# Expert stage of a transformer kernel: seven steps of 512 columns instead of fourteen of 256

## What is computed

```python
def moe_swiglu(h, w_router, w_gate, w_up, w_down):
    logits = jnp.einsum('bsd,de->bse', h, w_router).astype(jnp.float32)
    top_v, top_i = lax.top_k(logits, TOP_K)
    ...
        a = jnp.einsum('sd,edf->sef', hb, w_gate)
        u = jnp.einsum('sd,edf->sef', hb, w_up)
        act = jax.nn.silu(a) * u * gb[:, :, None]
        return jnp.einsum('sef,efd->sd', act, w_down)
```

## Time and profile before

| | us |
|---|---|
| median of 3 runs | 2570.42 |
| lowest and highest | 2569.68, 2573.59 |
| span of the profiled execution | 2562.5 |
| first to last turn of the expert stage | 725.6 to 1723.6 |

### The profile page before, as it was taken

One profiled execution on the slowest core, in us unless ns is written; L12 is line 12 of the kernel. 1 busy time (PEld: TensorE's weight loads), 2 busy tenths in 40 slices (PEclk: granted clock), 3 DMA queues, 4 the chain that ended last, 5 costly groups with the idle time before them and its releaser, 6 DMA issues. The chain is left out here.

```text
span 2562.5 us, 30519 instructions
## 1 busy us (share of the span) xinstructions
PE 2260.2 (88%) x11133; PEld 1876.1 (73%) x11133; DVE 1862.5 (73%) x1965; ACT 1343.6 (52%) x1446; POOL 54.4 (2%) x130
## 2 busy tenths in 40 slices
PE   3946899785799999999999999997879999787998
PEld 3825788673678888888887878776767878676786
DVE  6887667678589888888898888876645446555454
ACT  2423343352367777777777777763434435343443
POOL 2000000000000000000000000000000000000000
PEclk9957999896799999999999999997989999898999
DMA  8840678560179999999999999994424554231553
GB/s 297 284 156 2 211 282 289 213 208 1 49 242 349 352 348 354 351 353 349 353 348 350 344 349 346 347 344 143 157 82 148 196 175 150 99 116 66 175 174 134
DMA packets 412850, 595.07 MB, mean 232 GB/s; under 512 B 20316, under 2 KB 327751, under 8 KB 412743
## 3 DMA queue, kind: packets, MB, share of 16 engines
q1 hardware_dynamic: 407040, 586.55, 66.3%
q10 hardware_dynamic: 5702, 7.04, 0.8%
HBM read 592.47 MB, written 1.05 MB: 232 GB/s over the span
## 5 line engine op out<-in xcount | busy, mean ns | idle before, releaser
L136 PE MATMUL bank<-ring_rounded,hT_rounded 128*128 128x512 f32 (+3 forms) x944 | 373.8, 396 | 19.5 <-DVE ring_rounded L291 5.6
L693 DVE TENSOR_TENSOR ring_rounded<-ring,z_rounded 128x2048 fp32r<-128x2048 f32 x148 | 338.9, 2291 | 63.0 <-ACT z_rounded L685 61.3
L136 PE MATMUL bank<-ring_rounded,z_rounded 128*128 128x512 f32 x896 | 361.6, 404 | 3.0 <-DVE ats_rounded L2825 1.5
L693 DVE TENSOR_TENSOR ring_rounded<-ring,zT_rounded 128x2048 fp32r<-128x2048 f32 x145 | 332.3, 2292 | 42.2 <-ACT zT_rounded L685 40.8
L685 ACT ACTIVATE z_rounded<-ring 128x2048 fp32r<-128x2048 f32 x148 | 283.4, 1917 | 32.7 <-DMA ring<-in_moe_w_up 25.0
L685 ACT ACTIVATE zT_rounded<-ring 128x2048 fp32r<-128x2048 f32 x145 | 277.9, 1917 | 35.8 <-DMA ring<-in_moe_w_up 18.4
L136 PE MATMUL bank<-ring_rounded,L_rounded 128*128 128x512 f32 x712 | 282.3, 396 | 15.3 <-DVE ats_rounded L826 10.5
L137 PE MATMUL bank<-zT_rounded,ats_rounded 128*128 128x512 f32 x600 | 234.8, 391 | 0.0
L136 PEld LDWEIGHTS bank<-ring_rounded,hT_rounded 128*128 128x128 f32 x944 | 181.5, 192 | 56.0 <-issue 15.7
L136 PEld LDWEIGHTS bank<-ring_rounded,z_rounded 128*128 128x128 f32 x896 | 168.3, 188 | 41.7 <-DVE ring_rounded L693 4.3
L693 DVE TENSOR_TENSOR ring_rounded<-ring,PT_rounded 128x2048 fp32r<-128x2048 f32 x71 | 162.6, 2290 | 44.0 <-ACT PT_rounded L685 43.9
(11 more groups left out here) (491 smaller groups left out, 4876.5 us busy)
## 6 DMA issues: line engine op xcount, KB each, us to landing
ring<-in_moe_w_gate SPq DMA_DIRECT2D x224, 512.0 KB, 5.1
ring<-in_moe_w_up SPq DMA_DIRECT2D x224, 512.0 KB, 6.9
ring<-in_moe_w_down SPq DMA_DIRECT2D x224, 512.0 KB, 7.8
ring<-in_ffn_w_gate_up SPq DMA_DIRECT2D x88, 512.0 KB, 5.0
ring<-in_ffn_w_down SPq DMA_DIRECT2D x66, 512.0 KB, 7.8
ring<-in_w_ada SPq DMA_DIRECT2D x48, 512.0 KB, 6.6
ring<-in_w_in SPq DMA_DIRECT2D x32, 512.0 KB, 4.8
xn<-in_w_ada SPq DMA_DIRECT2D x24, 512.0 KB, 9.5
```

Of the source, the lines that this page charges most:

```text
L136: pe.matmul(out, r32(a[0]), r32(b[1]), start=start, stop=False, skip_group_check=True)
L693: dve.tensor_tensor(r32(w), w, high(hi), ALU.subtract).then_inc(sem_out, 1)
```

## The change

A step now covers 512 hidden columns, and there are seven per expert (56 in all, before 112). A step uses all six slots: 0 and 1 hold gate (four blocks of 128 rows, 512 columns each), 2 and 3 hold up, 4 and 5 hold two row blocks of `w_down` each. A row of a gate or up transfer is 2 KB long where it was 1 KB; a row of `w_down` stays 4 KB. PE's `into` replaces `gate_up`: gate goes to bank 6, up to bank 7, 24 products each, and the semaphore `gu` is raised once for each slot, `down` likewise. Since bank 7 also takes the transposed activation, `up` waits until that has been split (`actT`). SP waits for each slot alone. `turn` makes four transposes. The later gathers and the swap go to bank 6, so PE waits for silu before them, and for `hTb` (or `combined`) before the next gate products; they stand in steps 2 to 5 and 6 of seven. On DVE the low part of slot 0 of the next step stands ahead of the multiplication. The clearing of the output bank and the wait for `me_count` stand ahead of the first step. The loads of slots 4 and 5 of step m stand behind the four loads of step m + 1, for step 0 too. At the end, both last `w_down` slots are split behind the copy of the last turn. On PE all steps are written out; on ACT and DVE a loop runs over pairs of experts.

```diff
-MOE_STEPS = F_EXPERT // FT
+WIDE = 512
+MOE_STEPS = F_EXPERT // WIDE
+ROWS_DOWN = WIDE // P
...
+MOE_SLOTS = ('gu', 'gu', 'gu', 'gu', 'down', 'down')
+MOE_UP = 2
+MOE_ALL = MOE_STEPS * N_EXP
+def moe_use(s, m, after=0):
+    return m * (4 if s < 4 else 2) + (s % 4 + after)
...
         for a in range(2):
-            sp.dma_start(w[:, a:a + 1, :], c.moe_down[:, bass.ds(m * 2 + a, 1), :])\
+            sp.dma_start(w[:, a:a + 1, :], c.moe_down[:, bass.ds(m * ROWS_DOWN + (2 * half + a), 1), :])\
               .then_inc(sem, 16)
+    else:
+        w = w.rearrange('p (k n) -> p k n', k=4)
+        view = c.moe_gate if s < MOE_UP else c.moe_up
+        for a in (0, 2):
+            sp.dma_start(w[:, a:a + 2, :], view[:, bass.ds(e * KD + (4 * half + a), 2), bass.ds(i * WIDE, WIDE)])\
+              .then_inc(sem, 16)
...
+    def load(s, e, i, m, first=False):
         if not first:
-            sp.wait_ge(E['gu' if q < 2 else 'down'], m + (moe_before(p, 'gu') - 1))
+            sp.wait_ge(E[MOE_SLOTS[s]], moe_use(s, m, (-3 if s < 4 else -1) + moe_before(p, MOE_SLOTS[s])))
...
-        moe_load(c, sp, q, e, i, m, (j0 + 3 * r + q) % RING, (c.again if p else c.landed)[(j0 + 3 * r + q) % RING])
...
-    def step(e, i, r, m):
-        load(0, e, i, r, m)
-        load(1, e, i, r, m)
-        load(2, None, None, 1 - r, m - 1)
...
+    def step(e, i, m, first=False):
+        for s in range(4):
+            load(s, e, i, m)
+        for s in (4, 5):
+            load(s, None, None, m - 1, first)
+    for s in range(4):
+        load(s, 0, 0, 0, True)
+    step(0, 1, 1, True)
+    with sp.Fori(2, MOE_STEPS) as i:
+        step(0, i, i)
     with sp.Fori(1, N_EXP) as e:
...
-GATHER_STEP = MOE_STEPS - 6
+GATHER_STEP = 2
 GATHERS = 4
+SWAP_STEP = GATHER_STEP + GATHERS
...
-            body(i % 2, m0 + i, ahead, None if g > GATHERS else (lambda g=g: extra(e, half, g, last)))
-        if last:
-            end(e)
-            return
-        body(0, m0 + MOE_STEPS, 2, lambda: next_extra(e, half, known))
-        body(1, m0 + (MOE_STEPS + 1), 2, None)
-    for r in range(2):
-        body(r, r, 2, None)
+            more = (lambda g=g: extra(e, half, g, last)) if 0 <= g <= GATHERS else None
+            after = (lambda: boundary(e - 1, 1 - half, last)) if i == 0 and known != 0 else None
+            body(m0 + i, known == 0 and i == 0, not (last and i == MOE_STEPS - 1), more, after)
     moe_experts(eng, expert)
+    end()
...
 def later_gather(c):
-    return c.pb[7][:, S:2 * S]
+    return c.pb[6][:, 0:S]
...
-    def gate_up(half, r, m):
+    def into(first, out, half, m):
         hTe, hLe = c.hTe[half], c.hLe[half]
         for q in range(2):
-            pe.wait_ge(E['gu_lo'], moe_split_value(st, q, m, p))
...
+            wh, wl = parts(s, 4)
...
+                mm = product(pe, out[:, :], (hTe[:, x, :], hLe[:, x, :]), (wh[:, i, :], wl[:, i, :]), x == 0, x == KD - 1)
+            mm.then_inc(E['gu'], 1)
...
     def turn(m):
         pe.wait_ge(E['act'], m + (1 + moe_before(p, 'act')))
-        for a in range(2):
-            mm = pe.transpose(T[:, a * P:a * P + P], c.fa[:, 0, a * P:a * P + P], c.ident[:, :])
+        for a in range(ROWS_DOWN):
+            mm = pe.transpose(U[:, a * P:a * P + P], c.moe_fa[:, a * P:a * P + P], c.ident[:, :])
         mm.then_inc(E['turned'], 1)
...
-                             first and a == 0, last and a == 1)
-        mm.then_inc(E['down'], 1)
+        for q in range(2):
+            pe.wait_ge(E['down_lo'], moe_use(4 + q, m, 1 + moe_before(p, 'down_lo')))
+            wh, wl = parts(4 + q, 2)
+            for h in range(2):
+                col = slice(h * 512, h * 512 + 512)
+                for i in range(2):
+                    a = 2 * q + i
+                    mm = product(pe, c.pb[4 + h][:, :], (c.moe_faT[:, a, :], c.moe_faL[:, a, :]),
+                                 (wh[:, i, col], wl[:, i, col]), first and a == 0, last and a == ROWS_DOWN - 1)
+            mm.then_inc(E['down'], 1)
...
+    def swap(e):
...
         pe.wait_ge(E['sums'], e + (1 + moe_before(p, 'sums')))
...
     def expert(e, m0, half, known):
         last = known == N_EXP - 1
...
+        for i in range(MOE_STEPS):
+            m = m0 + i
+            if i == 0 and known != 0:
+                pe.wait_ge(E['hTb'], e * 4 + (4 + moe_before(p, 'hTb')))
+                pe.wait_ge(E['combined'], e + moe_before(p, 'combined'))
+            elif not last and 0 < i - GATHER_STEP <= GATHERS:
+                pe.wait_ge(E['hTb'], e * 4 + (4 + i - GATHER_STEP + moe_before(p, 'hTb')))
+            into(0, G, half, m)
+            if i or known != 0:
+                pe.wait_ge(E['actT'], m + moe_before(p, 'actT'))
+            into(MOE_UP, U, half, m)
             g = i - GATHER_STEP
-            gate_up(half, i % 2, m0 + i)
-            down(1 - i % 2, m0 + (i - 1), False, False)
...
-            turn(m0 + i)
+            if (0 <= g < GATHERS and not last) or g == GATHERS:
+                pe.wait_ge(E['silu'], m + (1 + moe_before(p, 'silu')))
+                if g < GATHERS:
+                    gather(e + 2, 1 - half, g, later_gather(c))
+                else:
+                    swap(e)
+            if i or known != 0:
+                if i == 1 and known != 0:
+                    scatter(e - 1)
+                down(m - 1, i == 1, i == 0)
+            turn(m)
         if last:
-            down(1, m0 + (MOE_STEPS - 1), False, True)
+            down(m, False, True)
             scatter(e)
-            return
-        m1 = m0 + MOE_STEPS
-        pe.wait_ge(E['hTb'], e * 4 + (8 + moe_before(p, 'hTb')))
-        gate_up(1 - half, 0, m1)
-        down(1, m0 + (MOE_STEPS - 1), False, True)
-        turn(m1)
-        gate_up(1 - half, 1, m0 + (MOE_STEPS + 1))
-        scatter(e)
...
+        gather(1, 0, g, first_gather(c, g))
     if p == 0:
         for n in range(NT):
             mm = pe.matmul(c.pb[3][:, 0:N_EXP], c.ones[:, 0:P], c.chosen[:, n, :], start=n == 0, stop=n == NT - 1)
         mm.then_inc(c.s['mo_tensor'], 1)
         moe_clear(c, pe, 2)
     pe.wait_ge(E['hTb'], 4 + moe_before(p, 'hTb'))
-    gate_up(0, 0, 0)
-    turn(0)
-    if p == 0:
-        pe.wait_ge(c.s['me_count'], 1)
-        moe_clear(c, pe, 3)
...
+    if p:
+        moe_experts(pe, expert)
+        return
+    pe.wait_ge(c.s['me_count'], 1)
+    moe_clear(c, pe, 3)
+    for e in range(N_EXP):
+        expert(e, e * MOE_STEPS, e % 2, e)
...
+    def body(m, first, ahead, extra, after):
+        if not first:
+            copyT(m - 1)
+        hi(3, m)
+        if not first:
+            hi(4, m - 1)
+        act.wait_ge(E['gu'], moe_use(MOE_UP, m, moe_before(p, 'gu')))
+        act.activation(c.moe_fs, c.pb[6][:, :], ACT.Silu).then_inc(E['silu'], 1)
+        if not first:
+            hi(5, m - 1)
         if ahead:
-            hi(1, 1 - r, m + 1)
-        act.wait_ge(E['turned'], m + (1 + moe_before(p, 'turned')))
+            hi(0, m + 1)
         if extra:
             extra()
-        act.activation(r32(c.faT[:, 0, :, :]), c.pb[7][:, 0:2 * P].rearrange('p (a t) -> p a t', a=2), ACT.Copy)\
-           .then_inc(E['T_hi'], 1)
-        hi(2, r, m)
-        if ahead == 2:
-            hi(0, r, m + 2)
+        if ahead:
+            hi(1, m + 1)
+            hi(2, m + 1)
+        if after:
+            after()
...
+    def end():
+        copyT(MOE_ALL - 1)
+        hi(4, MOE_ALL - 1)
+        hi(5, MOE_ALL - 1)
+        take_sum(N_EXP - 1)
+    for s in range(3):
+        hi(s, 0)
...
+    def body(m, first, ahead, extra, after):
+        if not first:
+            lowT(m - 1)
+        lo(3, m)
+        if not first:
+            lo(4, m - 1)
+            lo(5, m - 1)
+        if ahead:
+            lo(0, m + 1)
         dve.wait_ge(E['silu'], m + (1 + moe_before(p, 'silu')))
-        dve.tensor_tensor(c.fa[:, 0, :], c.fs[:, 0, :], c.pb[6][:, FT:2 * FT], ALU.mult).then_inc(E['act'], 1)
-        if ahead:
-            lo(1, 1 - r, m + 1)
-        dve.wait_ge(E['T_hi'], m + (1 + moe_before(p, 'T_hi')))
-        dve.tensor_tensor(r32(c.faL[:, 0, :, :]), c.pb[7][:, 0:2 * P].rearrange('p (a t) -> p a t', a=2),
-                          high(c.faT[:, 0, :, :]), ALU.subtract).then_inc(E['actT'], 1)
+        dve.wait_ge(E['gu'], moe_use(3, m, 1 + moe_before(p, 'gu')))
+        dve.tensor_tensor(c.moe_fa, c.moe_fs, c.pb[7][:, :], ALU.mult).then_inc(E['act'], 1)
         if extra:
             extra()
-        lo(2, r, m)
-        if ahead == 2:
-            lo(0, r, m + 2)
+        if ahead:
+            lo(1, m + 1)
+            lo(2, m + 1)
+        if after:
+            after()
```

More of the change, by code:

```diff
@@ new lines @@
+MOE_UP = 2
+MOE_ALL = MOE_STEPS * N_EXP
+def moe_use(s, m, after=0):
+    return m * (4 if s < 4 else 2) + (s % 4 + after)
+def moe_stage(core):
+    st = dict(kind='moe', j0=len(core.jobs))
+    for m in range(MOE_ALL):
+        for s, kind in enumerate(MOE_SLOTS):
+            job(core, None, (f'me_{kind}', moe_use(s, m, 1)))
+    return st
```

(47 more changed lines are left out.)

156 lines of the change are left out of this document (52 added, 104 removed).

## The result

The changed kernel takes 2551.68 us (median of 5 runs, 2545.41 to 2557.36) where the kernel before takes 2569.68 (5 runs, 2560.80 to 2573.59): a ratio of 0.9935, with an interval of 0.9918 to 0.9952. The profiled execution of after has a span of 2551.9 us and took 2553.62.

The account below looks back on a forecast made before the run. PE was taken as the bound, transfers close behind. 734.4 + 970.8 + 15.9 = 1721.1 plus 4 of waits, against 1733.9, gave -8.8: span 2562.5 to 2553.7, plus 7.9 makes 2561.6 us; range 2554 to 2577.

Parts of the forecast that it names:

- The bound: In the steps PE is the bound, transfers close behind; 17.0 us of PE waits, as late landings find no slack.
- The first rival: Transfers are the true bound, or loads land no earlier, so saved waits return: 2574.6 to 2577 us; chance 0.27 for both.
- Work and waits of the steps: New turn 0 to turn 55: 970.8 us of PE work plus 4 us of waits left.
- R: Waits left in the steps, 0 to 17.0 us; taken as 4: 2 experts' first steps, 1 start, 1 late landings.
- The waits behind the experts' first turns: Extra DVE operations leave the transposed part 0.7 us of slack; 0.3 us for each of seven steps, 2 us.
- The slack of the multiplication: In a clean step the multiplication is done at 14.1 us, the turn due at 16.35: slack 2.2 us.
- The end: Behind the last turn PE idles nearly 8 us, then the last `down` runs twelve products slow, twelve at full speed.
- t: Time of the last turn; the last `down` was to end at t + 15.9, or t + 18.5 at the low clock.
- The first turn: At the start, gate begins at 720.2 and the first turn, behind the multiplication, at 734.4 us.
- 7.9 us "above the span": The runs' median lies 7.9 us above the profiled span, so 2553.7 us of span becomes 2561.6.
- the old order had ten steps without a gather in a row: Clean steps might fall 0.3 us behind on transfers; the new order has only three per expert, and gather steps win 0.6 back.
- The slower rival: The multiplication behind the low part of slot 0 delays every turn, 0.5 us x 56 = 28, giving 2586 us; chance 0.15.

Follow-up runs that it names:

- singly: The kernel before with only its gate and up slots freed one by one; 2555.74 us, 0.9955; a second time (singly_again) 2552.94 us, 0.9952.
- after_again: The changed kernel unchanged, run and profiled a second time; 2550.87 us, 0.9933 of the kernel before.
- control: The kernel before, unchanged, run and profiled once more; 2567.5 us, ratio 1.0005.
- spread: The kernel before with steps 2 to 7 of each expert written out and the four gathers moved to steps 3, 6, 8 and 10 of fourteen; 1.0006.
- lateall: The changed kernel with the low part of slot 1 ahead of the multiplication on VectorE in every step; 2591.82 us, 1.0094 of the kernel before.
- pairs: The changed kernel with SyncE waiting for the second slot of each pair before loading either; 2586.32 us, 1.0063 of the kernel before.

## Why the prediction was off

**The bound: right.** The waits of before came from slots that were freed late, and with single slots they are gone; `singly` shows it with nothing else changed. The first rival, transfers as the true bound, falls with the same kernel: the same bytes in the same rows, 12.7 us sooner. So does the second half of that rival, that the loads would land no earlier.

**Work and waits of the steps: 974.8 us forecast, 971.5 and 973.3 measured.** Part of it is the work, which was 1.3 us too high: mostly because the clean step with the other set of token buffers takes 17.00 us, where 17.06 (2 x 8.54 less 0.02) was reckoned, and 28 steps stand on it. R was put at 4 us. By the shorter work it is 2.0 in after and 3.8 in `after_again`, of which 1.7 is the half clock behind the first turn, a term the prediction didn't have. The waits behind the experts' first turns, put at 2 us, are 0.8 and 1.8 us; there the slack was small, as forecast, and it didn't hold everywhere. The slack of the multiplication was put at 2.2 us and is 3.5 by the median. From issue to landing I had taken 5.9 us, from a slot issued together with its neighbour. In `after_again` the first gate slot of a step takes 5.0 to 7.8 us, with a median of 5.7, so one step said too little. The multiplication takes 0.68 us and not 0.74.

**The end: mis-sized by 1.5 us.** t + 15.9 was forecast; it ends at 1719.82 + 0.23, t + 14.4. PE was idle for 6.1 us and not nearly 8, as the load of slot 4 landed sooner: in `after_again` it is issued at t - 2.5 and split from t + 1.95, 4.5 us later, where the landing was forecast for t + 3.5. The two paces came as forecast (0.43 us a product, then 0.23).

**The first turn: 734.12 against 734.4, in part by luck.** The first gate product came 0.65 us later than forecast (720.85 against 720.2), and the turn followed it 0.9 us sooner (13.3 us against 14.2). These three together put the end of the last `down` at 1720.05 instead of 1725.1, and the gain of the profiled stage at 13.9 us instead of 8.8.

**The stretch behind the stage** was taken as unchanged. It took 3.1 us more in after than in before, and that hid most of the miss: the span was forecast as 2553.7 and is 2551.9.

**The step that failed most: 7.9 us "above the span".** I took the difference between the median of three runs and the profiled span for something that lies around every execution. In after the five runs exceed their own spans by 1.7 to 2.8 us. In the 65 runs of before made for the experiments it is 1.7 to 1.8 us. So before's profiled execution took some 2564.3, which lies below its median, and its three runs lay above it: over all 70 runs of before, control among them, the median is 2567.3 (2559.0 to 2577.6), over 11 of after 2551.4. A forecast of 2553.7 for the span means some 2556 for the run. Of the miss of 9.9 us in the time, 1.8 is in the span and 8.1 in this step: 6.2 because a run exceeds its span by 1.7 and not 7.9, and 1.9 because the median lies below the profiled run. A range that began 6 us lower would have held the result. The gain by the medians of all runs is 15.9 us, and the stage's is 14.4; where the rest lies is not shown.

**One argument was wrong and did no harm:** "the old order had ten steps without a gather in a row". `spread` breaks the row up and has the same waits. That the gathers' place gives slack back is not shown by any run.

**The slower rival** did not come, but its step is real: `lateall` and `pairs` both reach it, and are 41 and 35 us slower than after. It stood at 0.15 with a price of 28. That the price is near is luck: it was 0.5 us at each of 56 turns, and what was measured stands elsewhere. I had named the multiplication alone as its place; in `pairs` the transposed part costs more, and in `lateall` the gathered tokens do.

## What to carry to other kernels

In a ring of buffers, first look at when each slot is freed, not at how large the steps are: one semaphore per slot brought 12.7 of 14.4 us, while the new steps with slots freed in pairs lost 0.6%. For each operation in a hand-written order, write down by how much it is early, in each kind of step. Two operations here have some 3 us in most steps, and spend it when a slot comes one matrix later; the tightest place, the step behind an expert's first turn, pays first. Before a time is forecast from a profiled span, subtract the span from its own execution's time and from nothing else.

## What was not expected of the hardware

The code behind the stage is the same in all kernels, and TensorE's time in it is not. The windows view from the last `down` to the end, of control, after, after_again and singly:

```profile
1735.50:2565.00 829.50, 723.50 (x3784) 616.99 (x3782) 446.73 (x505) 349.54 (x450) 23.45 (x44) 0.94 0.41 139
1719.80:2551.90 832.10, 723.31 (x3784) 617.71 (x3782) 446.61 (x505) 349.54 (x450) 23.39 (x44) 0.94 0.42 140
1720.50:2547.90 827.40, 720.59 (x3784) 615.62 (x3782) 446.74 (x505) 349.16 (x450) 23.38 (x44) 0.95 0.42 141
1720.80:2557.90 837.10, 731.07 (x3784) 623.67 (x3782) 446.77 (x505) 349.03 (x450) 23.38 (x44) 0.93 0.41 138
```

With 3784 matmuls in each, PE is busy 720.6 to 731.1 us at a granted clock of 0.95 to 0.93, while DVE and ACT agree to 0.6 us. The stretch takes 827.4 to 837.9 us over the fourteen profiled executions. `singly` was profiled with 837.1 and `singly_again` with 829.8, the same code both times. The clock is not all of it: after takes 3.1 us more here than before does, with PE busy for only 0.6 us more. Where the lower grants fall is not settled by these runs. One profiled span of this kernel can be 5 us off for this stretch alone.
